# One output region goes through all three high/low passes before the next: order of matmuls in a two-layer trunk on one core

## The reference

```
D_MODEL = 1024
SEQ = 256
D_FF = 3584
N_EXPERTS = 8
TOP_K = 2
...
def swiglu(h, w_gate, w_up, w_down):
    return (jax.nn.silu(h @ w_gate) * (h @ w_up)) @ w_down

def moe_swiglu(h, w_router, w_gate, w_up, w_down):
    logits = (h @ w_router).astype(jnp.float32)
    top_vals, top_idx = lax.top_k(logits, TOP_K)
    gates = jax.nn.softmax(top_vals, axis=-1)
    comb = jnp.sum(jax.nn.one_hot(top_idx, N_EXPERTS, dtype=jnp.float32) * gates[..., None], axis=-2)
    out = jnp.zeros_like(h)
    for e in range(N_EXPERTS):
        out = out + comb[..., e:e + 1].astype(h.dtype) * swiglu(h, w_gate[e], w_up[e], w_down[e])
    return out
```

## Time and profile before

| | |
|---|---|
| median of 3 runs | 1544.58 us (1539.51 to 1548.32) |
| profiled execution: its own time | 1547.95 us |
| profiled execution: span | 1546.1 us |
| TensorE busy | 1474.3 us, 95% |
| VectorE busy | 1188.4 us, 77% |
| ScalarE busy | 931.7 us, 60% |
| mean granted TensorE clock | 0.975 of full speed |
| read from memory | 422.92 MB, 274 GB/s |

### The profile page before, as it was taken

How to read it: one execution, slowest core, us unless ns; L and a number is a source line. 1 busy time by engine, 2 the same in 40 slices (tenths; PEclk the granted TensorE clock), 3 DMA queues, 4 the chain that set the end, 5 groups by cost and what they waited for, 6 DMA issues and landing times.

```text
span 1546.1 us, 25783 instructions
## 1 busy us (share of the span) xinstructions
PE 1474.3 (95%) x10854; PEld 1352.8 (87%) x10854; DVE 1188.4 (77%) x1139; ACT 931.7 (60%) x916; POOL 39.3 (3%) x49
## 2 busy tenths in 40 slices
PE   4979999999997999999999999999999999999995
PEld 4879999998886999899889988988998898898883
DVE  6886555557545897888789889888888979888882
ACT  4844444343432776766767667667676767766761
POOL 2030000003000000000000000000000000000000
PEclk9989999999997999999999999999999999999996
DMA  8345555553214999999899999999999989988900
GB/s 314 143 173 195 191 189 181 181 186 137 82 51 195 358 356 342 339 359 371 302 373 365 339 345 361 336 351 353 339 337 362 373 331 348 359 336 346 361 20 29
DMA packets 59282, 425.64 MB, mean 275 GB/s; under 512 B 6944, under 2 KB 7072, under 8 KB 7840
## 3 DMA queue, kind: packets, MB, share of 16 engines
q1 hardware_dynamic: 58320, 422.60, 73.4%
q10 hardware_dynamic: 848, 1.39, 0.3%
HBM read 422.92 MB, written 1.05 MB: 274 GB/s over the span
## 4 chain that ended last, share of the span: by engine, by line
PE 89%; DVE 5%; ACT 3%; issue 1%; DMA 1%; POOL 1%; ACTq 0%; POOLq 0%; DVEq 0%
PE ps L1684 38%; PE ps L1706 20%; PE ps L1402 10%; PE ps L1424 5%; PE ps L1354 3%; PE ps L1654 2%; PE ps L1672 2%; PE ps L1467 2%; PE ps L1570 1%; PE ps L1691 1%; DVE w_lo L1201 1%; ACT w_hi L643 1%; DMA ring<-in_positions 1%; PE ps L1514 1%; DVE w_lo L786 1%
## 5 line engine op out<-in xcount | busy, mean ns | idle before, releaser
L1201 DVE TENSOR_TENSOR w_lo<-ring,w_hi 128x2048 fp32r<-128x2048 f32 x336 | 766.6, 2290 | 129.8 <-ACT w_hi L643 123.5
L643 ACT CAST w_hi<-ring 128x2048 fp32r<-128x2048 f32 x336 | 639.5, 1909 | 267.8 <-PE ps L1684 215.6
L1684 PE MATMUL ps<-w_hi,xg_hi 128*96 128x256 f32 x1792 | 248.2, 281 | 2.5 <-ACT w_hi L643 2.5
L1684 PE MATMUL ps<-w_lo,xg_hi 128*96 128x256 f32 x1792 | 243.6, 278 | 0.9 <-DVE w_lo L1201 0.2
L1684 PE MATMUL ps<-w_hi,xg_lo 128*96 128x256 f32 x1792 | 243.4, 278 | 0.0
L1684 PEld LDWEIGHTS ps<-w_hi,xg_hi 128*96 128x96 f32 x1792 | 222.8, 162 | 16.2 <-issue 2.6
L1684 PEld LDWEIGHTS ps<-w_lo,xg_hi 128*96 128x96 f32 x1792 | 216.5, 162 | 2.5 <-DVE w_lo L1201 2.5
L1684 PEld LDWEIGHTS ps<-w_hi,xg_lo 128*96 128x96 f32 x1792 | 217.4, 162 | 0.0
L786 DVE TENSOR_TENSOR w_lo<-ring,w_hi 128x2048 fp32r<-128x2048 f32 x64 | 147.5, 2309 | 82.2 <-ACT w_hi L456 82.1
L456 ACT CAST w_hi<-ring 128x2048 fp32r<-128x2048 f32 x64 | 121.9, 1905 | 143.8 <-PE ps L1402 92.4
L1706 PE MATMUL ps<-w_hi,ht_hi 128*96 128x512 f32 x448 | 128.1, 408 | 0.0
(11 more groups left out here) (268 smaller groups left out, 1381.2 us busy)
## 6 DMA issues: line engine op xcount, KB each, us to landing
ring<-in_moe_w_gate SPq DMA_DIRECT2D x112, 1024.0 KB, 5.6
ring<-in_moe_w_up SPq DMA_DIRECT2D x112, 1024.0 KB, 5.6
ring<-in_moe_w_down SPq DMA_DIRECT2D x112, 1024.0 KB, 5.6
ring<-in_ffn_w_gate SPq DMA_DIRECT2D x14, 1024.0 KB, 4.8
ring<-in_ffn_w_up SPq DMA_DIRECT2D x14, 1024.0 KB, 4.8
ring<-in_ffn_w_down SPq DMA_DIRECT2D x14, 1024.0 KB, 4.8
ring<-in_lru_w_in SPq DMA_DIRECT2D x8, 1024.0 KB, 11.6
ring<-in_attn_w_qkv SPq DMA_DIRECT2D x6, 1024.0 KB, 4.7
```

Source lines behind the costliest of these rows:

```text
L643: nc.scalar.copy(w_hi[:, (SPLITS + n) % PARTS], ring[:, s]).then_inc(hi_done, 1)
L1201: V.tensor_tensor(w_lo[:, part], ring[:, ORDER_MOE[n % SLOTS]], w_hi[:, part].bitcast(F32), ALU.subtract).then_inc(lo_done, 1)
L1684: mm = nc.tensor.matmul(ps[0:CAP, c % 2, m * CHF:(m + 1) * CHF], xs[a][:, k], w[b][:, k], start=(k == 0 and (a, b) == (0, 0)), stop=(k == ...
```

## The change

In `ffn_gate_up` the loop over the two regions f goes outside and the passes inside. In `ffn_down` every down product has the order that only the last had, and waits for the low part ahead of its first matmul. In the experts' `down` the loop over the two regions g goes outside, then the passes, then f. The number of matmuls and their operands stay.

```diff
--- before.py
+++ after.py
@@ -1392,10 +1392,10 @@
             def ffn_gate_up(what, c):
                 j, m = FFN_AT[what, c], int(what == "up")
                 w = [a.rearrange("p (k c) -> p k c", k=KC) for a in ffn_parts(j)]
-                for a, b in PASSES:
-                    if b:
-                        pe.wait_ge(*low_done(LRU_SPLITS + j))
-                    for f in range(2):
+                for f in range(2):
+                    for a, b in PASSES:
+                        if b and f == 0:
+                            pe.wait_ge(*low_done(LRU_SPLITS + j))
                         for k in range(KC):
                             if j == 0 and f == 0 and b == 0:
                                 pe.wait_ge(u_ready if a else u_hi_ready, k + 1)
@@ -1410,14 +1410,8 @@
                 w = [a.rearrange("p (f d) -> p f d", f=2) for a in ffn_parts(j)]
                 fs = (f_hi, f_lo)
                 last = c == NCH - 1
-                if last:
-                    pe.wait_ge(*low_done(LRU_SPLITS + j))
-                    order = [(a, b, d) for d in range(KC) for a, b in PASSES]
-                else:
-                    order = [(a, b, d) for a, b in PASSES for d in range(KC)]
-                for a, b, d in order:
-                    if b and not last and d == 0:
-                        pe.wait_ge(*low_done(LRU_SPLITS + j))
+                pe.wait_ge(*low_done(LRU_SPLITS + j))
+                for a, b, d in [(a, b, d) for d in range(KC) for a, b in PASSES]:
                     for f in range(2):
                         if (a, b) == (0, 0) and d == 0:
                             pe.wait_ge(f_ready, 2 * c + f + 1)
@@ -1698,14 +1692,13 @@
                 if c == 0:
                     pe.wait_ge(y_staged, 2 * i + 1)
                 hs = (ht_hi, ht_lo)
-                for a, b in PASSES:
-                    if b:
+                for g, a, b in [(g, a, b) for g in range(2) for a, b in PASSES]:
+                    if b and g == 0:
                         low_part(i, n)
                     for f in range(2):
-                        for g in range(2):
-                            mm = nc.tensor.matmul(ps[0:CAP, 2 + g, :], hs[a][:, c % 2, f], w[b][:, f, g * 512:(g + 1) * 512],
-                                                  start=(c == 0 and f == 0 and (a, b) == (0, 0)),
-                                                  stop=(c == NCH - 1 and f == 1 and b == 1))
+                        mm = nc.tensor.matmul(ps[0:CAP, 2 + g, :], hs[a][:, c % 2, f], w[b][:, f, g * 512:(g + 1) * 512],
+                                              start=(c == 0 and f == 0 and (a, b) == (0, 0)),
+                                              stop=(c == NCH - 1 and f == 1 and b == 1))
                 mm.then_inc(parts_used, 1)
 
             def lead(i):
```

## The result

| | before | changed |
|---|---|---|
| median of 15 runs | 1545.81 us | 1549.20 us |
| lowest to highest | 1538.71 to 1548.32 | 1544.52 to 1552.66 |
| ratio | | 1.0029, 95% interval 1.0017 to 1.0041 |
| profiled execution: own time | 1547.95 us | 1547.13 us |
| profiled execution: span | 1546.1 us | 1545.3 us |

What follows compares the result with a forecast made beforehand. TensorE, busy 1474.3 of 1546.1 us, was taken to bound the kernel. Waits of 5.3 + 1.0 = 6.3 us, rate 0, on 1547.95 gave 1554.3 us (ratio 1.004), or 1551 on the median; range 1540 to 1561.

Steps and rivals of the forecast that it cites:

- the waits' price: Experts' down products: low parts late at the first of experts 1 to 7 (5.3 us) and near the end (1.0): 6.3 us.
- a low wait beyond the eight: Sign of a wrong forecast: TensorE waiting for a low part anywhere but at eight named down products.
- Dense part: Dense feed-forward: earlier waits for low parts cost 0; its length changing by over 1 us would show the forecast wrong.
- The cover of 6.8 us: Dense down products: low part complete 6.8 us or more before their first matmul, at all 14.
- The down products' rate: Experts' 512-column down products: change of rate taken as 0, with 5 us kept to both sides.
- the change of bank: Down products: if switching banks made matmuls 17 ns longer, 21 us gained and 1530 us; 256-column rows spoke against it.
- the repeated stationary block: Down products: the second matmul of a pair already reloads its block, so ending such pairs loses nothing.
- the prediction's own sign, 5 ns a matmul: Forecast wrong if the down products' own rate moves by more than 5 ns a matmul.
- The mix of levels: Experts' gate and up pieces: 119 quick and 105 slow, expected to stay near these numbers; taken as 0.
- The quick level throughout: Rival: TensorE stays quick after down products, in experts and dense part; 1530 us, or half of it, 1537; chance 0.13.
- The slow level throughout: Rival: all the experts' gate and up pieces run slow, beside the waits; 1560 to 1565 us; chance 0.20.
- The unpaid wait: Rival: at the experts' down products the low part comes early enough, so no wait is paid; 1545 us; chance 0.17.

Runs made afterwards that it cites:

- e2: Changed kernel with the experts' down products back in the old order, so only the dense feed-forward is new; ratio 1.0001 to the kernel before.
- e10: Changed kernel without the four bf16 matmuls of zeros that clear banks 4 to 7; ratio 0.9963 to the kernel before.
- e8: Kernel before without the four bf16 matmuls of zeros that clear banks 4 to 7; ratio 0.9941.
- e4: Kernel before with the two inner loops, f and g, exchanged in the experts' down products, passes still outside; ratio 0.9979.
- e6: Experts' down products ordered bank, f, then passes high-high, high by w_lo, low-high, low part read second; 1555.53 us in one run.

## Why the prediction was right

- *Where it happens, and the waits' price: right.* 7 x 0.77 + 1.0 + 0.1 = 6.5 us measured against 7 x 0.76 + 1.0 = 6.3. The places and lengths came out as worked out from the low part's end and the due time. The prediction had taken a low wait beyond the eight as a sign of being wrong, and there is a ninth, at the last down product; but it is under 0.1 us, and the margin there was put at 0.11. That the low part's own time doesn't move with TensorE held too.
- *Dense part: right.* The cover of 6.8 us held, and the new order costs nothing at the slow level (changed kernel, e2) and at the quick one (e10).
- *The down products' rate: the term taken as 0 was -3.0 us.* It lay within the bounds of 5 us to both sides. With it the sum is 6.3 - 3.0 = 3.3 us, and 4.5 (2.6 to 6.3 by the interval) were measured; 6.3 alone is at the interval's upper end. So the waits were foreseen and this gain was not. The prediction had looked at the change of bank. What the time goes with is the repeated stationary block, and it named that only to say that nothing is lost by it; that conclusion from the earlier trace rows was wrong. The trace of before held the hint, in the 4 ns that the steps within a pair take longer than the others. By the prediction's own sign, 5 ns a matmul, the rate didn't move: 29 ns are 2.4 ns a matmul.
- *The mix of levels: 115 slow gate and up pieces instead of 105*, by 0.08 us: 0.8 us. Whether the change has a part in it isn't shown: kernels with the old order of the down products had 96, 105, 106 and 112, the others 102 to 127, each in one execution. In the experts' stage 6.5 - 3.0 + 0.8 = 4.3 of the 5.2 us are named; the rest isn't.
- *Rivals.* The quick level throughout didn't come; in the dense part the order doesn't touch the level (e2, e10). e8 shows that such a state can be had, by another edit, and is worth what that rival had for the dense part. The slow level throughout didn't come either. The unpaid wait was wrong: in every kernel that reads the low part ninth, the margin was 0.27 to 0.32 us at all seven places, too little for a matmul that comes 0.92 us earlier.

## What to carry to other kernels

Before a consumer is made to read an operand earlier, compare the time at which that operand is complete with the new due time, at the tightest place and not on average: here 103 of 112 places had room, and the nine others decided. Changing the stationary block at every matmul saved 3 us here and cost nothing, and it could be had without moving any wait (e4). And when the same matmul has two rates in one trace, look at what stood right ahead of the first slow one: here four small matmuls cost 9 us.

## What the runs showed of the hardware that was not expected

- An order in which two matmuls of 512 columns in a row have the same stationary block takes longer than one in which they never have: a down product of 12 takes 2.849 us with six such pairs, 2.843 with four, and 2.820 to 2.821 with none, whatever the number of changes of bank (1, 5 or 10). Whether the block does it, or the weights' half that is repeated with it, is open.
- Four bf16 matmuls with one row of zeros shift all later matmuls of 256 columns from 113 to 118 ns, at the same granted clock, and the shift lasts for 215 us of uninterrupted work. Why, and why single zero matmuls in the attention part are sometimes followed by the quick rate, is open. In the experts the rate changes without such a matmul, but not anywhere: 36 of the 37 changes in the kernel before, and 48 of 51 in the changed one, are between the up piece of one chunk and the gate piece of the next, where the transposes and a down product stand. In e6 experts 2 to 7 have the same pattern of slow and quick pieces, piece by piece, so it isn't chance. What in it turns the rate is open.
